# Scoring key tiles in pairs: one exponential over two PSUM banks in differential attention

## What is computed

```
def diff_attention(q, k, v, lam):              # 8 heads, two 64-wide maps per head
    s = einsum("bqhmd,bkhmd->bhmqk", qi, k) * Dh ** -0.5
    p = softmax(s, axis=-1)                    # m = 0, 1: two maps
    a = p[:, :, 0] - lam * p[:, :, 1]
    return einsum("bhqk,bkhe->bqhe", a, v)     # 128-wide values
...
o = rmsnorm(diff_attention(q, k, v, lam), g_subln) * (1 - lam_init)
```

## Time and profile before

| | |
|---|---|
| median of 2 runs | 5415.15 us (5367.81 and 5462.49) |
| the profiled execution, its own time | 5363.21 us |
| span of its slowest core (core 5) | 5361.6 us |
| other cores' spans | 5306.8 to 5354.0 us |
| matmuls on TensorE (PE) | 3699.7 us busy, 69% of the span |
| ScalarE (ACT) | 2447.9 us busy, 46% |
| VectorE (DVE) | 1916.9 us busy, 36% |
| exponentials of the attention | 2656 instructions, 1327.2 us busy |
| chain that ended last | PE 50%, DVE 16%, ACT 12%, DMA 11%, issue 9% |

### The profile page before, as it was taken

The page is one execution under the profiler, slowest core; times in us unless marked ns, Lnnn a source line. Parts: engine busy times, 40 slices in busy tenths (PEclk is TensorE's granted clock), DMA queues, the critical chain, the costliest instruction groups (busy, mean ns, idle before and its releaser), DMA issues.

```text
span 5361.6 us, 96696 instructions; the slowest of 8 cores (5306.8 to 5361.6 us)
## 1 busy us (share of the span) xinstructions
PE 3699.7 (69%) x31892; PEld 2568.5 (48%) x31892; DVE 1916.9 (36%) x5172; ACT 2447.9 (46%) x5603; POOL 255.0 (5%) x335
## 2 busy tenths in 40 slices
PE   2444566666277777696976966966966967967966
PEld 1222343434155555464644644644644645745743
DVE  2332344444244441313144144153153152152155
ACT  1322333333111116493934934935835736736722
POOL 0111000000011110000000000000000000000000
PEclk8666677777688888797988988988988977877877
DMA  7778434443633235433343343343343443343333
GB/s 222 247 228 273 173 138 157 144 151 141 177 92 81 74 82 197 155 136 136 136 140 147 123 161 131 118 172 138 120 164 129 145 157 123 134 154 122 135 137 130
DMA packets 172934, 793.55 MB, mean 148 GB/s; under 512 B 14624, under 2 KB 43808, under 8 KB 104096
## 3 DMA queue, kind: packets, MB, share of 16 engines
q1 hardware_dynamic: 155600, 708.04, 38.5%
q0 software_dynamic: 16848, 79.32, 4.5%
HBM read 707.99 MB, written 79.31 MB: 147 GB/s over the span
## 4 chain that ended last, share of the span: by engine, by line
PE 50%; DVE 16%; ACT 12%; DMA 11%; issue 9%; DVEq 1%; POOL 1%; ACTq 0%; SPq 0%; POOLq 0%
PE B L289 50%; DVE tmp L289 9%; ACT tmp L289 4%; DMA ring<-Wscr 3%; DVE hT L289 3%; DMA KVbuf<-w_up 2%; ACT pT L289 2%; ACT st L289 2%; ACT L289 1%; ACT junk L289 1%; DMA KVbuf<-w_ada 1%; ACT ring L289 1%; DVEq L126 1%; DMA Vscr<-vloc 1%; DVE h2T L289 1%
## 5 line engine op out<-in xcount | busy, mean ns | idle before, releaser
L289 ACT ACTIVATE pT<-B 128x512 bf16<-128x512 f32 (+1 forms) x2656 | 1327.2, 574 | 345.9 <-PE B L289 337.6
L289 PE MATMUL B<-KVbuf,pT 128*128 128x129 bf16 x9792 | 1006.7, 224 | 101.9 <-ACT pT L289 68.3
L289 PE MATMUL B<-qm,KVbuf 128*128 128x256 bf16 (+1 forms) x5184 | 978.0, 277 | 50.1 <-DVE tmp L289 49.8
L289 PE MATMUL B<-hT,ring 128*128 128x256 bf16 (+1 forms) x5792 | 772.3, 304 | 237.6 <-DVE hT L289 110.2
L289 PEld LDWEIGHTS B<-KVbuf,pT 128*128 128x128 bf16 x9792 | 626.2, 98 | 472.5 <-issue 272.2
L289 PEld LDWEIGHTS B<-hT,ring 128*128 128x128 bf16 x5792 | 620.7, 110 | 384.5 <-issue 254.4
L289 PE MATMUL B<-h2T,ring 128*128 128x256 bf16 (+1 forms) x5632 | 667.4, 276 | 170.5 <-POOL ring L289 46.3
L289 PEld LDWEIGHTS B<-h2T,ring 128*128 128x128 bf16 x5632 | 503.2, 108 | 359.6 <-issue 232.3
L289 ACT ACTIVATE tmp<-tmp 128x256 f32<-128x256 f32 (+1 forms) x805 | 317.0, 395 | 766.3 <-DVE tmp L289 734.8
L289 PE MATMUL B<-ring,zT 128*128 128x512 bf16 x1056 | 317.4, 429 | 286.1 <-DVE zT L289 264.9
L289 DVE SCALAR_TENSOR_TENSOR tmp<-B,cw,tmp 128x255 f32<-128x255 f32 (+1 forms) x880 | 331.5, 377 | 353.3 <-ACT tmp L289 194.6
(11 more groups left out here) (109 smaller groups left out, 3045.8 us busy)
## 6 DMA issues: line engine op xcount, KB each, us to landing
ring<-Wscr SPq DMA_DIRECT2D x352, 1024.0 KB, 7.0
KVbuf<-Vscr SPq DMA_DIRECT2D x72, 1170.0 KB, 8.3
KVbuf<-Kscr SPq DMA_DIRECT2D x72, 1152.0 KB, 5.3
Wscr<-ring POOLq DMA_DIRECT2D x36, 1024.0 KB, 9.6
xsl<-xs SPq DMA_DIRECT2D x49, 512.0 KB, 7.1
KVbuf<-w_ada SPq DMA_DIRECT2D x12, 2048.0 KB, 14.1
KVbuf<-w_in SPq DMA_DIRECT2D x12, 2048.0 KB, 16.5
KVbuf<-w_up SPq DMA_DIRECT2D x22, 1024.0 KB, 8.7
```

The source lines that it names most:

```text
L289: return S.op(eng, lambda e: getattr(e, meth)(**kw), reads, writes)
```

## The change

Key tiles are handled in pairs. PSUM banks 1 and 2 become one tensor of 1024 columns (`B12`), banks 3 and 4 another (`B34`). `scores(kp)` writes the scores of two key tiles, four matmuls, into one of these two pairs of banks, and one exponential on 128x1024 elements reads both banks. The scores of one pair are issued ahead instead of those of two tiles. `pT` has three buffers of twice the size in place of four. Since banks 1 to 4 now hold scores, all heads accumulate in banks 5 and 6, and stage 0 of the end of a head is issued right after that head, ahead of the next one. The later stages are issued at pairs 1, 2, 3, 4 and 6. To make room in SBUF the ring of temporary tiles has 7 in place of 8.

```
-    pT = [A("pT%d" % i, [128, 2, T], BF16) for i in range(4)]
+    pT = [A("pT%d" % i, [128, 2, 2, T], BF16) for i in range(3)]
...
-    NTMP = 8
+    NTMP = 7
...
+    B12 = nc.alloc_psum_tensor("B12", [128, 1024], F32)
+    B34 = nc.alloc_psum_tensor("B34", [128, 1024], F32)
+    PB = [B0f, B12[:, 0:512], B12[:, 512:1024], B34[:, 0:512], B34[:, 512:1024]] + [nc.alloc_psum_tensor("B%d" % i, [128, 512], F32) for i in range(5, 8)]
+    BB = {1: B12, 3: B34}
...
-    SB = [3, 4, 7]
-
     def attention_head(h, Tn, nt, KT_ap, kkeys, V_of, vkeys, nkt):
-        par = h % 2
-        pbi = [5, 6] if par == 0 else [1, 2]
-
-        def scores(kt):
-            si = SB[nxt("ps", 3)]
-            ps, psk = PB[si], "B%d" % si
-            for m in range(2):
-                O("pe", "matmul", kkeys + [("qm", h)], [psk], out=ps[:, m * Tn:(m + 1) * Tn], lhsT=KT_ap[:, kt * 128:(kt + 1) * 128],
-                  rhs=qm[:, h, m, 0:Tn], start=True, stop=True)
-            return ps, psk
+        pbi = [5, 6]
+        nkp = nkt // 2
+
+        def scores(kp):
+            b0 = [1, 3][nxt("ps", 2)]
+            for j in range(2):
+                kt = 2 * kp + j
+                for m in range(2):
+                    O("pe", "matmul", kkeys + [("qm", h)], ["B%d" % (b0 + j)], out=PB[b0 + j][:, m * 256:m * 256 + Tn],
+                      lhsT=KT_ap[:, kt * 128:(kt + 1) * 128], rhs=qm[:, h, m, 0:Tn], start=True, stop=True)
+            return b0
 
         pend = [scores(0)]
-        if nkt > 1:
-            pend.append(scores(1))
-        stages = {1: 0, 4: 1, 6: 2, 8: 3, 10: 4, 13: 5}
-        for kt in range(nkt):
-            ps, psk = pend.pop(0)
-            if kt + 2 < nkt:
-                pend.append(scores(kt + 2))
-            pi = nxt("pT", 4)
-            O("act", "activation", [psk], [("pT", pi)], out=pT[pi][:, :, 0:Tn], in_=ps[:, 0:2 * Tn].rearrange("p (m t) -> p m t", m=2),
-              func=AF.Exp, scale=0.125)
...
+        stages = {1: 1, 2: 2, 3: 3, 4: 4, 6: 5}
+        for kp in range(nkp):
+            b0 = pend.pop(0)
+            if kp + 1 < nkp:
+                pend.append(scores(kp + 1))
+            pi = nxt("pT", 3)
+            O("act", "activation", ["B%d" % b0, "B%d" % (b0 + 1)], [("pT", pi)], out=pT[pi][:, :, :, 0:Tn],
+              in_=BB[b0][:, :].rearrange("p (j m t) -> p j m t", j=2, m=2)[:, :, :, 0:Tn], func=AF.Exp, scale=0.125)
+            for j in range(2):
+                kt = 2 * kp + j
+                for s in range(nt):
+                    for m in range(2):
+                        O("pe", "matmul", vkeys + [("pT", pi)], ["B%d" % pbi[s]], out=PB[pbi[s]][:, m * 129:(m + 1) * 129],
+                          lhsT=pT[pi][:, j, m, s * 128:(s + 1) * 128], rhs=V_of(kt), start=(kt == 0 and m == 0), stop=(kt == nkt - 1 and m == 1))
...
     def attention_fin(h, nt, stage):
         par = h % 2
-        pbi = [5, 6] if par == 0 else [1, 2]
+        pbi = [5, 6]
...
+            attention_fin(h, nt, 0)
-        for stg_ in range(6):
+        for stg_ in range(1, 6):
             attention_fin(NH - 1, nt, stg_)
```

More of the change, by code:

```diff
@@ L271, in build_program @@
     wsT = A("wsT", [128, 4, 128], BF16)
-    wsTf = tmps[7][:, :].rearrange("p (g q) -> p g q", g=4)
+    wsTf = tmps[5][:, :].rearrange("p (g q) -> p g q", g=4)
     lamt = tmps[6][:, 0:256].rearrange("p (a b) -> p a b", a=4)
@@ L283, in build_program @@
     B0 = B0f[:, :].bitcast(BF16).rearrange("p (a b) -> p a b", a=8)
-    PB = [B0f] + [nc.alloc_psum_tensor("B%d" % i, [128, 512], F32) for i in range(1, 8)]
+    B12 = nc.alloc_psum_tensor("B12", [128, 1024], F32)
+    B34 = nc.alloc_psum_tensor("B34", [128, 1024], F32)
+    PB = [B0f, B12[:, 0:512], B12[:, 512:1024], B34[:, 0:512], B34[:, 512:1024]] + [nc.alloc_psum_tensor("B%d" % i, [128, 512], F32) for i in range(5, 8)]
+    BB = {1: B12, 3: B34}
     KLOC = [("kloc", h) for h in range(8)]
@@ L355, in phase0 @@
         dma("sp", gsg[:], gsguF, [], ["gsg"], cst)
-        dma("sp", wsTf, w_sT, [], [("tmp", 7)], cst)
+        dma("sp", wsTf, w_sT, [], [("tmp", 5)], cst)
         dma("sp", bsb[:].rearrange("p g q -> p (g q)"), b_s.partition_broadcast(128), [], ["bsb"], cst)
@@ L376, in phase0 @@
                   scalar1=cslf[:, kc, ci:ci + 1], scalar2=None, op0=ALU.mult)
-        O("dve", "tensor_copy", [("tmp", 7)], ["wsT"], out=wsT[:], in_=wsTf)
+        O("dve", "tensor_copy", [("tmp", 5)], ["wsT"], out=wsT[:], in_=wsTf)
         O("dve", "tensor_scalar", ["gsb"], ["gsb"], out=gsb[:], in0=gsb[:], scalar1=(1.0 - LAM_INIT) * 0.5, scalar2=None, op0=ALU.mult)
@@ L490, in gelu2 @@
         O("dve", "scalar_tensor_tensor", [k0, skey], dkeys, out=dst, in0=t0[:, 0:n], scalar=1.0, in1=src, op0=ALU.add, op1=ALU.mult)
-    SB = [3, 4, 7]
     def attention_head(h, Tn, nt, KT_ap, kkeys, V_of, vkeys, nkt):
-        par = h % 2
-        pbi = [5, 6] if par == 0 else [1, 2]
-        def scores(kt):
-            si = SB[nxt("ps", 3)]
-            ps, psk = PB[si], "B%d" % si
-            for m in range(2):
-                O("pe", "matmul", kkeys + [("qm", h)], [psk], out=ps[:, m * Tn:(m + 1) * Tn], lhsT=KT_ap[:, kt * 128:(kt + 1) * 128],
-                  rhs=qm[:, h, m, 0:Tn], start=True, stop=True)
-            return ps, psk
-        pend = [scores(0)]
-        if nkt > 1:
-            pend.append(scores(1))
-        stages = {1: 0, 4: 1, 6: 2, 8: 3, 10: 4, 13: 5}
-        for kt in range(nkt):
-            ps, psk = pend.pop(0)
-            if kt + 2 < nkt:
-                pend.append(scores(kt + 2))
-            pi = nxt("pT", 4)
-            O("act", "activation", [psk], [("pT", pi)], out=pT[pi][:, :, 0:Tn], in_=ps[:, 0:2 * Tn].rearrange("p (m t) -> p m t", m=2),
-              func=AF.Exp, scale=0.125)
[L517 to L520, removed]
@@ L521, in attention_head @@
             if h >= 1:
                 for kk, stg_ in stages.items():
-                    if kt == min(kk, nkt - 1):
+                    if kp == min(kk, nkp - 1):
                         attention_fin(h - 1, nt, stg_)
@@ L682, in mixer @@
         S.mark('m_gmlp')
-        pmset[0] = [1]
+        pmset[0] = [7]
         for h in range(NH):
```

## The result

The changed kernel is slower. Its median is 5559.45 us (11 runs, 5506.77 to 5756.81) beside 5479.31 us before (10 runs, 5317.74 to 5547.08). Both sets hold executions in which one die or both ran at a lower granted clock; the ratio leaves those out and is **1.034, 95% interval 1.028 to 1.039**. The profiled execution took 5520.65 us.

What follows compares the result with a forecast made beforehand. The prediction took the loop through ScalarE and TensorE, not either engine's rate, to bound sample attention. Terms of 173 + 8 + 10 = 191 us on the profiled 5363 gave 5554 us, range 5485 to 5645, lower end drawn at 5475.

Steps and rivals of the forecast that it cites:

- Late tiles at clock 0.81: Two of eight sample tiles at the lower granted clock: a head 24.6 us against 21.3, adding 8 us.
- way back C': From an exponential's end through TensorE to the exponential reusing its banks: 1.34 us, against 0.90 before.
- spacing of pairs: Inside a sample-tile head, pair exponentials start (1.03 + 1.34)/2 = 1.185 us apart, 0.59 per key tile against 0.508.
- wait for VectorE's second block: At a head's start, value matmuls wait for VectorE to finish the last head's accumulators: 0.43 us, bounds nothing and 0.55.
- stages 1 to 3 on ScalarE, net: End-of-head stages pushing exponentials apart, partly hidden in ScalarE's idle time: 0.3 us a head, ends 0 and 1.13.
- one head: A sample-tile head summed to 22.95 us against 20.2; after 0.05 off for disturbances, 2.7 x 64 = +173 us.
- small tile: Tile with one query block: 18 pairs cost 0.8 us more, the boundary about 0.4; 8 heads, +10 us.
- prompt cycle: Prompt tiles keep 4.87 us a head, adding 0; +10 us if the pair's exponential comes into the cycle.
- Rival 1: ScalarE sets the pace after all: head 18.8 us, kernel 5275 us, 1.7% faster; chance 0.05.
- Rival 2: The loop is shorter than added up, added matmuls partly hidden: some 5450 us, within 2%; chance 0.08.
- Rival 3: TensorE's clock falls in sample attention: a head some 32 us, the kernel 6100 us; chance 0.03.
- The rule that spoke for the change: One exponential for two saves 93 ns a pair; over 1152 pairs 107 us less, if ScalarE were the limit.

Runs made afterwards that it cites:

- x5_pair_alt: Changed kernel with accumulators alternating between heads again (banks 5 and 6, then 7 and 0); 5493 us, ratio 1.032 to the kernel before.
- x4_pair_early: Changed kernel with the scores of the pair after next issued ahead of the current pair's value matmuls; 5315 us, ratio 0.989 to the kernel before.
- x1_two_tiles: Kernel before with two score banks instead of three, scores of one tile issued ahead, nothing paired; 6002 us, median of 3.
- x10_single_flat_late: Against the kernel before: four score banks, single tiles issued four ahead across heads, scores before values, alternating accumulators, stages later; 5211 us, ratio 0.979.

## Why the prediction came out as it did

The direction, the mechanism and the time inside a head held. **The step that failed** is the term "Late tiles at clock 0.81" of the sum, and with it the ground that the sum stands on: I took the granted clock of one execution, in two of its eight tiles, for a property of the kernel. The runs show 23.05 us a head at 0.97 to 0.99 in every tile, where the term had 24.6 for two of them.

| step | forecast | measured |
|---|---|---|
| exponential of a pair | 1.03 | 1.022 |
| way back C', idle between heads | 1.34 | 1.35 |
| spacing of pairs | 1.185 | 1.185 |
| wait for VectorE's second block | 0.43 | 0.37, by x5_pair_alt |
| stages 1 to 3 on ScalarE, net | 0.3 | about 0.4 |
| one head | 22.95 | 23.05 |
| eight sample tiles | +173 | +171 on core 2 |
| small tile, a head | +1.2 | +0.7 |
| late tiles, a head | 24.6 | 23.05, no late tile at 0.81 |
| small tile, whole | +10 | +1 on core 2, up to +8 on others |
| prompt cycle | 4.87 | 4.87 |

The stages' 0.4 is what is left of a head: 0.92 + 16 x 1.185 + 2.37 + 0.37 = 22.62 of 23.05. The +171 are from the first to the last exponential of each sample tile on core 2, 1312.4 us before and 1483.7 after. Of the rest of core 2's 179, the small tile has 1, the prompt attention 3 less than before, and the stages between the attentions 10 more; what made these longer is not shown.

**The term that was mis-sized most** is "Late tiles at clock 0.81". I carried two tiles over at 24.6 us a head. In the profiled execution after, every sample tile had 0.97 to 0.99 and 23.05 a head, also on core 4, the slowest. Against my 24.6 that is 1.55 x 16 = 25 us, most of the 33 by which 5554 is above 5520.65. No trace of the changed kernel has a sample tile at 0.81, so the 24.6 itself stays untested. Taken against the profiled execution before, the forecast was +191 and the measured +157; the ratio of 1.034 stands against my 191/5363 = 3.6%. The clock of single stretches is not a property of the kernel to be carried over: another run of the same changed kernel has cores at 0.82, and another all at 0.85. I should have forecast from core 2 and put the clock into the range alone.

**The small tile** was too dear by 9 us on core 2. Its heads grew by 0.7 and not 1.2. Its first interval between heads shrank from 22.97 to 18.99 on core 2, but that is no gain: TensorE waited 4.18 us in it for the values instead of 8.85, and 6.18 for the keys ahead of it instead of 2.02. On cores 5 and 6 the interval grew, and over the eight cores the tile became 1 to 8 us longer.

**The baseline.** I counted from 5363 and named 1% between it and the median. Beside the changed kernel, before had a median of 5479, again another one. That 5554 lies near the new median of 5559.45 is luck in part: the two medians lie only 80 us apart, less than half of my 191, because six of the ten executions before took 5462 us or more and the median falls near them, while five of the eleven after took 5607 or more and theirs does not. At like clocks the change costs 3.4%, some 180 us. An absolute time forecast from one execution is no better than that; a ratio is.

**The range.** The ends that I list add up to -52 and +143, 5502 to 5697; the stated 5485 to 5645 does not follow from them. The terms of one head add up to 22.97 and not 22.95, which changes nothing.

**The rivals.** Rival 1, ScalarE's pace, needed C' below 0.77. It did not come true in the change; x4_pair_early comes nearest, with C' = 2 x 0.963 - 1.02 = 0.90. Rival 2 needed a hidden part in the way back: C' was 1.35 and nothing hid. Rival 3, the clock: it stayed at 0.97 to 0.99 in the sample tiles, with TensorE idle for 0.2 us in every second pair.

The rule that spoke for the change, in the Trainium skill, "ScalarE: Activation LUTs", section "What ACT_TABLE_LOAD costs", gives an ACTIVATE of 1024 columns, by an estimate from its figures, 186 + 853 = 1039 ns; the trace has 1022 and agrees within 2%. Its saving did not show here, since ScalarE was not the limit. Where ScalarE nearly is, it shows in part: 18.29 us a head with pairs against 18.66 without.

## What to carry to other kernels

When two engines both look nine tenths busy, compute the loop: the time of one step on the one, plus the way back through the other, over the number of buffers. Here the piece was doubled and three buffers became two; that lengthened the way back by the added work of TensorE, 0.45 us a pair, and lost more than the fixed cost saved. Then look at what stands in the way back and could be issued behind the work that the other engine waits for: with the scores moved ahead of the values, the change went from 3.4% slower to 1.1% faster.

## What the hardware showed that I had not expected

In x1_two_tiles the small tile ran through at a granted clock of 0.50, the level of 1.2 GHz, on core 5, and a later sample tile at 1.00:

```profile
2080.00:2270.00 190.00, 159.80 (x1150) 101.99 (x1151) 11.92 (x47) 111.55 (x315) 0.00 (x0) 0.50 0.30 114
2720.00:2930.00 210.00, 151.92 (x1634) 97.33 (x1634) 20.00 (x84) 156.77 (x326) 0.00 (x0) 1.00 0.23 87
```

On core 4 the small tile was for 17 us at 1.00 and then fell to 0.50 for the rest of it; the two stretches, and TensorE in the first of them:

```profile
2084.00:2100.00 16.00, 9.68 (x116) 6.96 (x116) 0.94 (x4) 9.34 (x29) 0.00 (x0) 1.00 0.18 61
2101.00:2260.00 159.00, 138.59 (x987) 87.22 (x987) 9.70 (x38) 95.81 (x271) 0.00 (x0) 0.50 0.28 106
2089.22 0.27 PE L289 MATMUL B<-KVbuf,pT 128*128 128x129 bf16 x2 [0.40 <-ACT pT L289]
2090.28 0.27 PE L289 MATMUL B<-KVbuf,pT 128*128 128x129 bf16 x2 [0.40 <-ACT pT L289]
```

Before it fell, TensorE was busy 9.68 of 16 us, with gaps of 0.4 us after every second exponential. The changed kernel's small tile, busy 88.08 of 116 us, stayed at 0.98; every other kernel's small tile has 0.80 or more. While the clock was up, two key tiles took 2090.28 - 2089.22 = 1.06 us, 19 us a head, as the loop says; the 23.5 are the lower clock's. So the danger of rival 3 is real, with two buffers of one tile.

The lengths of ScalarE's records also misled: with four tiles ahead in x10_single_flat_late an exponential's record is 1111 ns long on average at a spacing of 0.48 to 0.49 us, against 598 before at 0.50. The work is the same, so the records seem to hold waiting time too, and only the distance between starts is a rate.
